# Experts stage of a mixture-of-experts layer: the top expert gets a second block on the same weights, the overflow block goes, and three down buffers and two halved loads come in

## The reference

```python
N_EXPERTS, D_EXPERT, TOP_K = 32, 512, 2
def hierarchical_moe(h, w_group, b_group, w_expert, b_expert, w_gate, w_up, w_down):
    pg = softmax(xt @ w_group + b_group)            # 4 groups, the best one is taken
    le = (xt @ w_expert + b_expert)[group]          # 8 experts in it, the best two
    gates = g_prob * e_prob
    # every expert e computes, on the rows (tokens) that chose it:
    #   (silu(xb @ w_gate[e]) * (xb @ w_up[e])) @ w_down[e]
    # rows are multiplied by their gate and added up per token
```

## Time and profile before

| | us |
|---|---|
| median of 3 runs | 4357.59 |
| lowest, highest | 4355.55, 4358.58 |
| the profiled execution's own time | 4350.82 |
| its span, first to last instruction | 4349.0 |
| PE busy | 3894.6 (90%) |
| experts stage of layer 0, about | 2374 to 2927 |
| experts stage of layer 1, about | 3741 to 4293 |

### The profile page before, as it was taken

One profiled execution on the slowest core, in us unless ns is written; L12 is line 12 of the kernel. 1 busy time (PEld: TensorE's weight loads), 2 busy tenths in 40 slices (PEclk: granted clock), 3 DMA queues, 4 the chain that ended last, 5 costly groups with the idle time before them and its releaser, 6 DMA issues. The chain is left out here.

```text
span 4349.0 us, 78912 instructions
## 1 busy us (share of the span) xinstructions
PE 3894.6 (90%) x34318; PEld 2403.2 (55%) x34318; DVE 2108.5 (48%) x3081; ACT 1007.0 (23%) x1749; POOL 624.2 (14%) x460
## 2 busy tenths in 40 slices
PE   7999998899989998999996999866999999699973
PEld 4555654455556545566544666543666665466642
DVE  3565356455545554555555222215667777422214
ACT  2333223133331221222210000003445541000002
POOL 2322011032211100000001211100311300211111
PEclk9999999999999999999997999987999999799986
DMA  3233202332320243545423999982000121699996
GB/s 127 98 102 100 66 20 88 92 105 93 105 90 30 88 126 107 90 80 86 93 89 110 415 421 409 420 362 88 16 1 16 40 78 74 246 421 414 415 421 271
DMA packets 260372, 707.86 MB, mean 163 GB/s; under 512 B 59467, under 2 KB 185555, under 8 KB 234551
## 3 DMA queue, kind: packets, MB, share of 16 engines
q1 hardware_dynamic: 245447, 658.11, 42.4%
q0 software_dynamic: 13248, 40.38, 2.5%
q10 hardware_dynamic: 1328, 4.24, 0.3%
HBM read 630.32 MB, written 63.82 MB: 160 GB/s over the span
## 5 line engine op out<-in xcount | busy, mean ns | idle before, releaser
L2707 DVE TENSOR_TENSOR sb_work<-sb_work,ps 128x384 f32<-128x384 f32 (+2 forms) x66 | 34.2, 518 | 714.1 <-ACT sb_work L2694 714.1
L512 PE MATMUL ps<-sb_mixT,sb_work 128*128 128x512 f32 x768 | 358.9, 605 | 8.6 <-ACT sb_x_tok L854 5.5
L512 PE MATMUL ps<-sb_xT,sb_work 128*128 128x512 f32 x768 | 357.2, 602 | 8.6 <-ACT sb_x_tok L854 5.5
L2694 ACT ACTIVATE sb_work<-ps 128x384 f32<-128x384 f32 (+2 forms) x66 | 30.4, 461 | 1046.5 <-PE ps L2664 1046.5
L1664 PE MATMUL ps<-sb_xT,sb_work 128*128 128x512 f32 x512 | 236.2, 600 | 0.0
L2664 PE MATMUL ps<-sb_work,sb_mixT 128*32 128x256 f32 x3264 | 191.3, 396 | 47.1 <-DMA sb_work<-moe_w_up 37.7
L2664 PE MATMUL ps<-sb_work,sb_xT 128*32 128x256 f32 x3264 | 194.0, 401 | 36.8 <-DMA sb_work<-moe_w_up 27.4
L512 PEld LDWEIGHTS ps<-sb_mixT,sb_work 128*128 128x128 f32 x768 | 138.5, 192 | 148.7 <-issue 131.9
L512 PEld LDWEIGHTS ps<-sb_xT,sb_work 128*128 128x128 f32 x768 | 137.9, 191 | 147.7 <-issue 130.9
L2151 DVE TENSOR_REDUCE sb_cols<-ps 128x1 f32<-128x1024 f32 x128 | 150.6, 1218 | 85.9 <-PE ps L1994 85.7
L2664 PEld LDWEIGHTS ps<-sb_work,sb_mixT 128*32 128x32 f32 x3264 | 126.2, 115 | 111.6 <-issue 55.5
(11 more groups left out here) (493 smaller groups left out, 7144.2 us busy)
## 6 DMA issues: line engine op xcount, KB each, us to landing
sb_work<-moe_w_gate SPq DMA_DIRECT2D x34, 2048.0 KB, 14.3
sb_work<-moe_w_up SPq DMA_DIRECT2D x34, 2048.0 KB, 19.2
sb_work<-moe_w_down SPq DMA_DIRECT2D x32, 2048.0 KB
sb_mixT<-moe_w_down SPq DMA_DIRECT2D x17, 2048.0 KB, 7.7
sb_xT<-moe_w_down SPq DMA_DIRECT2D x17, 2048.0 KB, 8.3
sb_xT<-moe_w_gate SPq DMA_DIRECT2D x16, 2048.0 KB, 17.2
sb_xT<-moe_w_up SPq DMA_DIRECT2D x16, 2048.0 KB, 21.6
sb_mixT<-moe_w_gate SPq DMA_DIRECT2D x16, 2048.0 KB, 17.0
```

Source lines behind the costliest of these rows:

```text
L512: last = pe.matmul(m.ps[:, bank, :], b.w[i][:, k, :], m.xT[:, k, half * HALF:(half + 1) * HALF], start=(k == 0), stop=(k == NK - 1))
L2694: act.activation(b.act[n % 2][:, 0:strips[n], :], strip_sums(2 + 2 * (n % 2))[:, 0:strips[n], 0:P], ACT.Silu).then_inc(silued, 1)
L2707: dve.tensor_tensor(act, act, strip_sums(2 + 2 * (n % 2))[:, 0:strips[n], P:2 * P], ALU.mult).then_inc(multiplied, 1)
```

## The change

Block 32 is no overflow block any more. It has two strips and takes the rows of the largest ranked expert (block 2, `SHARED`) beyond its 128; it runs in the turn right after block 2 with the same weights. Rows that still don't fit go to the loop of overflow blocks. So there are 33 turns as before but 32 weight loads (`LOADS`, `TURNS`, `WEIGHTS`), and 88 strips. The order is now 0, 1, 6 to 17, then 2, 32, 18, 3, 19, 4, 20, 5, then 21 to 31.

There are three down buffers, and down weights of loads 0 and 1 are fetched in the routing stage. The product runs over k outermost and strips inside; of the loads 2 and 31 each of gate and up comes in two halves of four k-chunks (1 MiB), and the product waits for each half. The first half of load 2 goes out when half of product 0 is done. Small buffers move to other places, which makes room, and the routing's vector code changes with the blocks. In `combine_stage` SP waits for tile 1's gathers before it loads the projection weights.

```diff
+SHARED, EXTRA = N_FIRST, N_EXPERTS
 N_FIXED = N_EXPERTS + 1
+N_BLOCKS = N_FIXED + OVERFLOW
 def strips_of(block):
-    if block >= N_EXPERTS:
+    if block == EXTRA:
+        return 2
+    if block >= N_FIXED:
         return 4
+def weights_in_turn():
+    order, turns, weights = blocks_in_turn(), [], []
+    for w, block in enumerate(order):
+        turns += [block, EXTRA] if block == SHARED else [block]
+        weights += [w, w] if block == SHARED else [w]
+    return order, turns, weights
+LOADS, TURNS, WEIGHTS = weights_in_turn()
+HALVED = (2, N_EXPERTS - 1)
+def last_use(n):
+    return n + 1 == len(WEIGHTS) or WEIGHTS[n + 1] != WEIGHTS[n]
...
+            sp.wait_ge(turned, 2 * NT)
+            load_down(1, a["moe_w_down_2"][l, 1])
             sp.wait_ge(logits_ready, NT)
-            sp.dma_start(experts.down[0], by_rows(a["moe_w_down_2"][l, 0])).then_inc(
-                expert_loaded, 16)
-            sp.wait_ge(expert_loaded, 80)
+            load_down(0, a["moe_w_down_2"][l, 0])
+            sp.wait_ge(expert_loaded, 96)
...
-            def skip_places(dst, at, n, spare, least):
-                do(dve.tensor_scalar(spare, at, N_FIRST - 0.5, None, ALU.is_lt))
+            def skip_strips(dst, spare, at, n):
+                do(dve.tensor_scalar(spare, at, float(SHARED), 2.0 - P // STRIP, ALU.is_equal, ALU.mult))
+                do(dve.scalar_tensor_tensor(spare, at, N_FIRST - 0.5, spare, ALU.is_lt, ALU.add))
                 do(dve.scalar_tensor_tensor(spare, at, MIDDLE_BLOCKS - 0.5, spare, ALU.is_gt, ALU.add))
                 do(dve.scalar_tensor_tensor(spare, at, WIDE_BLOCKS - 0.5, spare, ALU.is_gt, ALU.add))
-                do(dve.scalar_tensor_tensor(dst, spare, float(STRIP), n, ALU.mult, ALU.add))
-                do(dve.scalar_tensor_tensor(spare, dst, least - 0.5, spare, ALU.is_gt, ALU.mult))
                 do(dve.scalar_tensor_tensor(dst, spare, float(STRIP), n, ALU.mult, ALU.add))
...
-            do(dve.scalar_tensor_tensor(place, over_q, -float(P), place, ALU.mult, ALU.add))
             do(dve.tensor_scalar(over, over_q, 0.0, None, ALU.is_gt))
+            do(dve.scalar_tensor_tensor(spare_c, over_q, -float(P // STRIP), spare_c, ALU.mult, ALU.add))
+            do(dve.tensor_tensor(spare_c, spare_c, over, ALU.mult))
+            do(dve.scalar_tensor_tensor(place, spare_c, float(STRIP), rank, ALU.mult, ALU.add))
+            do(dve.tensor_scalar(extra, place, P - 0.5, None, ALU.is_gt))
+            do(dve.scalar_tensor_tensor(place, extra, -float(P), place, ALU.mult, ALU.add))
...
+            do(dve.scalar_tensor_tensor(slot, extra, float(EXTRA - SHARED), slot, ALU.mult, ALU.add))
...
-    b.down = [k4(here[:, 0:4 * SEQ]), k4(work[:, 0:4 * SEQ])]
+    b.down = [k4(here[:, 0:4 * SEQ]), k4(work[:, 8 * SEQ:12 * SEQ]), k4(work[:, 4 * SEQ:8 * SEQ])]
...
-            if loaded(n, 0):
-                pe.wait_ge(*loaded(n, 0))
-            for g in range(strips[n]):
-                for k in range(NK):
-                    for j in range(QUARTERS):
-                        last = pe.matmul(strip_sums(2 + 2 * (n % 2), tile[j])[:, g, :], b.x_turned[n % 2][:, g, k, :],
-                                         b.gate_up[n % 2][:, :, k, j * P:(j + 1) * P], start=(k == 0), stop=(k == NK - 1))
-            last.then_inc(up_ready, 1)
+            for half in range(2):
+                if loaded(n, 0, half):
+                    pe.wait_ge(*loaded(n, 0, half))
+                for k in range(half * NK // 2, (half + 1) * NK // 2):
+                    for g in range(strips[n]):
+                        for j in range(QUARTERS):
+                            last = pe.matmul(strip_sums(2 + 2 * (n % 2), tile[j])[:, g, :], b.x_turned[n % 2][:, g, k, :],
+                                             b.gate_up[weights[n] % 2][:, :, k, j * P:(j + 1) * P],
+                                             start=(k == 0 and g % 2 == 0),
+                                             stop=(k == NK - 1 and (g % 2 == 1 or g == strips[n] - 1)))
+                last.then_inc((half_used, up_ready)[half], 1)
...
+            def load_gate_up(w):
+                sources = [by_rows(source(w, name)) for name in ("gate", "up")]
+                if w not in HALVED:
+                    for part in range(2):
+                        sp.dma_start(b.gate_up[w % 2][:, part, :, :], sources[part]).then_inc(gate_up_loaded[w % 2], 16)
+                    return
+                for half, landed in enumerate((gate_up_loaded[w % 2], second_loaded)):
+                    k = slice(half * NK // 2, (half + 1) * NK // 2)
+                    if w == HALVED[0]:
+                        sp.wait_ge((half_used, up_ready)[half], 1)
+                    for part in range(2):
+                        sp.dma_start(b.gate_up[w % 2][:, part, k, :], sources[part][:, k, :]).then_inc(landed, 16)
...
+            gate_up_used(0)
             for n in range(N_FIXED):
-                if n + 3 < N_FIXED:
-                    sp.wait_ge(up_ready, n + 2)
-                    load_gate_up(n + 3)
+                if n + 1 < N_FIXED:
+                    gate_up_used(n + 1)
                 sp.wait_ge(y_ready, n + 1)
-                if n + 2 < N_FIXED:
-                    load_down(n + 2)
+                if last_use(n) and WEIGHTS[n] + 3 < N_EXPERTS:
+                    load_down(WEIGHTS[n] + 3)
...
             if out is None:
+                sp.wait_ge(gathered[1], 32)
                 load_group_weights(sp, first_weights, group_buffers(m).w, 0, first_loaded)
```

More of the change, by code:

```diff
@@ L2256, in out_route_stage @@
     NL = N_GROUPS + N_EXPERTS
-    early, late = [11 * SEQ], [0]
+    areas = {"early": m.v_tok[:].rearrange("p a n -> p (a n)"), "late": m.work[:, 0:4 * SEQ],
+             "last": m.const[:, K_LEVEL:K_IOTA]}
+    early, late, last = (["early", 0], ["late", 0], ["last", 0])
     def take(at, *shape):
         n = int(np.prod(shape))
-        view = m.work[:, at[0]:at[0] + n]
-        at[0] += n
-        assert at[0] <= (12 if at is early else 5) * SEQ
+        view = areas[at[0]][:, at[1]:at[1] + n]
+        at[1] += n
+        assert at[1] <= areas[at[0]].shape[1]
         return view.rearrange("p (a b) -> p a b", b=shape[1]) if len(shape) == 2 else view
@@ L2276, in out_route_stage @@
     more, ends, starts, counts, at_block, spare_e = (take(late, N_EXPERTS) for _ in range(6))
-    at_choice, spare_c = (take(late, pairs) for _ in range(2))
+    at_choice, spare_c, extra = (take(late, pairs) for _ in range(3))
     larger, before = take(late, N_EXPERTS, N_EXPERTS), take(early, N_EXPERTS)
-    blocks = take(late, pairs, N_BLOCKS)
-    slot_tokens, quarter = take(late, N_BLOCKS), take(early, 1)
-    compare, ids = larger[:, 0:OVERFLOW, :], take(late, OVERFLOW)
-    places = m.work[:, 5 * SEQ:5 * SEQ + pairs * P].rearrange("p (a b) -> p a b", b=P)
+    blocks = take(last, pairs, N_BLOCKS)
+    slot_tokens, quarter = take(last, N_BLOCKS), take(early, 1)
+    compare, ids = larger[:, 0:OVERFLOW, :], take(last, OVERFLOW)
+    places = m.spare[:, 0:pairs * P].rearrange("p (a b) -> p a b", b=P)
     iota = m.const[:, K_IOTA:K_IOTA + P]
@@ L2671, in down @@
                 pe.wait_ge(y_copied, n - 1)
[L2672 to L2673 removed]
+            if loaded(n, 1, 0):
+                pe.wait_ge(*loaded(n, 1, 0))
             for g in range(strips[n]):
@@ L2820, in _ @@
                     def _(sp):
-                        expert = sp.value_load(m.overflow[0:1, bass.ds(o + later, 1)], min_val=0, max_val=N_EXPERTS - 1)
-                        load_expert(sp, m, a, l, b, 0, expert, loads[0])
+                        expert = sp.value_load(m.overflow[0:1, bass.ds(o, 1)], min_val=0, max_val=N_EXPERTS - 1)
+                        load_expert(sp, m, a, l, b, 0, expert, (gate_up_loaded[0], down_loaded[0]))
                         sp.wait_ge(y_copied, 1)
@@ L2835, in _ @@
                         pool.sem_inc(tokens_ready, 1)
-                    expert_engines(nc, m, block, b, [4], lambda n, part: (loads[0][part], (32, 16)[part]),
+                    expert_engines(nc, m, block, b, [4], [0], lambda n, part, half: ((gate_up_loaded, down_loaded)[part][0], (32, 16)[part]),
                                    lambda n: (tokens_ready, 1))
```

85 lines of the change are left out of this document (44 added, 41 removed).

## The result

| | before | after |
|---|---|---|
| median of 5 runs each, us | 4357.4 | 4332.7 |
| lowest to highest | 4355.55 to 4358.58 | 4331.33 to 4336.46 |
| the profiled execution's own time, its span | 4350.82, 4349.0 | 4336.46, 4334.6 |

The ratio is 0.9944, 95% interval 0.9933 to 0.9955: faster by 24.7 us. I had forecast 41.4, so 16.7 us are missing, and 4332.7 lies 1.7 us above the upper end of my range (4331). The two profiled executions differ by 14.4 only; the one of before was short (4350.82, under all of its other runs) and the one of after long. That turned out to matter for more than the offset.

What follows compares the result with a forecast made beforehand. Weight transfers were taken to bound the experts stages, a queue ending with the last gate and up weights. Terms summed to 19.6 us per layer, 39.2 for two, 41.4 with the combine: 4357.6 - 41.4 = 4316 us, range 4303 to 4331.

Steps and rivals of the forecast that it cites:

- Part 1: Experts stage: one expert's loads and two strips fewer take 16.2 us per layer off the transfer queue.
- Part 4: Third load in halves, starting during the first product: 0.5 us per layer, bounds 0 and 5.
- Part 5: Last load in halves, product starting on the first half: 3.5 us per layer, bounds 0 and 3.6.
- Part 2: Shared turn: queue has 31.6 us of work against PE's 31.9, so cost 0, bounds 0 and 6.6 us per layer.
- rival B: Queue runs dry in the shared turn (6.6 us per layer), last half gains nothing (3.5): 4336 us; chance 0.13.
- Part 3: Down ring of three and second down tensor fetched in routing: gain 0, other bound 5.0 us per layer.
- Part 6: Gate and up products with k outermost: effect 0; a 10% slowdown would cost about 6 us per layer.
- rival C: k outermost slows PE by a fifth or more in the products: 4345 to 4355 us; chance 0.05.
- Parts 7 to 9: Routing's extra vector instructions cost 0.6 us per layer; SP's earlier expert-number reads and clear_overflow's two extra blocks cost nothing.
- Part 10: Layer 0's combine: projection weights loaded after tile 1's gathers save 2.2 us, bounds 0 and 2.5.
- The offset: Median of runs 6.8 us above the profiled execution's 4350.8, assumed to stay after the change.
- signs of being wrong: Experts stage shortening under 14 or over 25 us; also expected: 45 to 50 us of PE waits, 10.5 us three-strip products.

Runs made afterwards that it cites:

- e13: The kernel after without the second block: block 32 not gathered, multiplied or stored; gain over before 39.8 us, ratio 0.9909.
- e5: The kernel before, unchanged, run once more for a second trace; time 4356.8 us, span 4355.0.
- e11: The kernel after with the second expert's down weights loaded at the start of the experts stage, not in the routing stage; gain over before 24.4 us, ratio 0.9943.
- e12: The kernel after with the third gate and up weights loaded whole after the first product; gain over before 24.7 us, ratio 0.9942.
- e8: The kernel after with each layer's last gate and up weights loaded whole, the third load still in halves; gain over before 15.0 us, ratio 0.9964.
- e1: The kernel after with strips outermost again in gate and up products, except the first and the two with halved weights; gain over before 24.7 us, ratio 0.9941.
- e2: The kernel before with only k put outermost in the gate and up products; gain over before 0.7 us, ratio 0.9998.
- e4: The kernel after with every product in two halves of k, strips outside k within each half; gain over before 25.5 us, ratio 0.9941.
- e7: The kernel after without SP's wait for tile 1's rows ahead of the projection weights in layer 0's combine; gain over before 24.7 us, ratio 0.9946.
- e15: The kernel after with all loads from the third on in halves and the top expert in the last wide place; gain over before 36.0 us, ratio 0.9917.
- e14: The kernel after with every gate and up load from the third on in halves, the first released in mid product; gain over before 28.7 us, ratio 0.9934.

## Why the prediction was wrong

- **Part 1, one load fewer: right in kind, its size perhaps too large.** With the shared turn out of the way (e13) layer 0's stage runs from the first product at 2376.75 to the last take at 2906.75, 530.0 us; usual before (e5) from 2373.97 to 2923.45, 549.5 (rows below). The 19.5 us between answer to my parts 1, 4 and 5 and the two strips left out: 16.2 + 0.5 + 3.5 + 1.2 = 21.4. With 4.8 for part 5 and nothing for part 4, as measured, 13.5 are left for part 1; the gain of e13 leaves 14.4. No run tests part 1 by itself.

DVE's last take in e5, and PE's first product and DVE's last take in e13:

```profile
2923.45 0.69 DVE L2720 TENSOR_TENSOR sb_work<-ps,sb_work 128x512 f32<-128x512 f32 x1 [2.76 <-PE ps L2677]
```

```profile
2376.75 2.79 PE L2694 MATMUL ps<-sb_work,sb_mixT 128*32 128x256 f32 x24 [9.46 <-DVE sb_mixT L2734]
...
2906.75 0.69 DVE L2752 TENSOR_TENSOR sb_work<-ps,sb_rows 128x512 f32<-128x512 f32 x1 [2.76 <-PE ps L2709]
```

- **Part 2, the shared turn at 0: the step that failed.** It costs 6.3 us per layer, all but my upper bound of 6.6. Two things in the count of what the queue has (31.6 us against 31.9, and the 31.9 were 33.7 in after) were wrong. The backlog of 6.6 us was read from one wait of 1.24 us in an execution whose early turns were 1.4 us faster than usual. And the count added up transfers without asking when each is issued: the second of the two down tensors goes out only 26.6 us in. What went out before it are gate, up and one down tensor, 15.0 us; with stores, gathers and whatever backlog there was the queue lasted 20 us, so at most 5 of them were backlog, and for the next 6.6 it had little to do. I wrote in rival B that 31.6 against 31.9 is no margin, and gave it 0.13. Rival B was right in this half of it, and wrong in the other, that the last halves gain nothing.
- **Part 3, ring and prefetch at 0: right** (e11). The third down buffer by itself was not tried.
- **Part 4, early halves at 0.5: right** within the error (e12). The DMA share of 0.65 in 2400 to 2410 fits the limit that I named, the second product's end.
- **Part 5, last halves at 3.5: under the truth,** 4.8 per layer (e8). The 7.1 us of the last product were again those of the first trace; in e5 it waited 4.72 us and took 8.80, and from there to the last take it is 15.8 us, after 10.6. The Trainium skill ("TensorE: Matmul & The Clock Gate", "Loop structure matters more than you think") made me keep the low clock in the second half as the lower bound. Its bad case is a long wait ahead of every matmul, and that is not what the halves have: after the one wait of 1.03 us in mid product the second half took 3.66 us, as the first did. The whole product behind a wait of 3.06 us ran slow, as the page has it.
- **Part 6, k outermost at 0: right** (e1, e2, e4), though after's trace first looked like rival C.
- **Parts 7 to 9:** the first product of layer 0 starts at 2376.49, before at 2376.25 and, in e5, at 2373.97. Too small to tell. Part 9 was not tested.
- **Part 10, the combine at 2.2: wrong.** The 2.2 (3.0 in the trace) appear where I looked, at the first vector instruction, and 2.8 are gone 32 us later. I called the weights' first use covered; by the 1.33 us ahead of it it was not. The other 1.27 us are the low clock of the first projection, which e7 has as well.
- **The offset.** I carried over 6.8 us between profiled execution and median. The traces of after and e5 show that the first profiled execution was the odd one. The forecast does not suffer from the offset, but from two readings of that trace, the backlog and the 7.1 us of the last product. The 55.3 us of waits and the 10.5 us of a product, also read there, misled only my signs of being wrong.
- **A small misreading:** slice 35 has 246 GB/s and slice 25 409; the plateaus of 410 to 421 that I named are slices 23, 24, 26 and 36 to 39.

With the measured sizes the sum is 2 x (16.2 - 6.3 + 4.8 - 0.6) + 0.2 = 28.4, with 24.7 measured. The 3.7 us between are not placed; they are within what the intervals allow. Since the prices of the shared turn and of the last halves are themselves differences to after, what is left over falls on part 1, the smaller ones, or chance.

## What to carry over

Work that holds on to a prefetch buffer for two turns has to be paid out of the queue's backlog, and where transfers and compute run at one pace, as here, there is next to none. Write down when each transfer of that time can be issued, not only how many bytes they are; start with a backlog of zero, and take a nonzero one only from a wait that a second trace shows as well. When the profiled execution lies outside the range of the timed runs, its margins of a microsecond are not those of the kernel. A transfer moved behind a gather wins at the gather's consumer; follow it to its own first use before the gain is booked.

## What was not expected of the hardware

- The same kernel's early turns took 15.5 us in one execution and 16.6 to 16.9 in another. The difference is a pause or slower stretch of about 1.2 us in each three-strip product, with nothing that the profile shows ahead of it. It is in all 16 other traces (after and e1 to e15), whatever the order of the matmuls. At about the same moment SP issues a down load and four stores, DVE scales a row of tokens and POOL issues a gather, but these stand there in the one trace without the pause too. Its cause is open. Before's two stages are 4.2 and 2.6 us longer with it (e5 against the first trace), 6.8 us in all.
- In e14 28 more pairs of gate and up tensors per layer went out as two transfers of 1 MB each, 56 transfers more, and the total did not rise (28.7 us gained, after 24.7); the window 2400 to 2410 has a share of 1.01 at 412 GB/s. The Trainium skill ("DMA: Bandwidth & Descriptors", "Anatomy of one DMA") has a fixed 2 us for each transfer, there for those that GpSimd issues; the weights here are issued by SyncE. An estimate with that figure is 112 us per layer if paid in turn; no such cost is in the run, so in a full queue it lies beside other transfers or is not there.
